# Four column groups in the mixed stage, four kinds of projections with the weights stationary, modulation chunks of 2048 rows, and the mixer's small steps at new tile numbers

## The chip, the cores and the metric

The kernel runs on one core of a Trainium2 chip. The metric is the device time of one execution in microseconds (us). TensorE (PE) multiplies, VectorE (DVE), ScalarE (ACT) and GpSimd (POOL) do the rest, and the queues of SyncE (SP) and POOL start the DMA transfers.

## What is computed

Two blocks over x (256 positions, 2048 channels), all in float32. Only the first one is touched by the change:

```python
mod = silu(c) @ w_ada + b_ada                 # w_ada is 2048 x 12288
sh1, sc1, gt1, sh2, sc2, gt2 = split(mod, 6)
h = rmsnorm(x, g_mix) * (1 + sc1) + sh1
z = h @ w_in                                  # pool, q, k, v, forget logits, lru x, lru y
y = concat(pool_mixer(zp), forgetting_attention(zq, zk, zv, zf), rg_lru_branch(zx, zy))
x = x + gt1 * (y @ w_out)
h = rmsnorm(x, g_ffn) * (1 + sc2) + sh2
x = x + gt2 * conv_glu_ffn(h)
```

The pool mixer is a banded product over positions and a map of each group; the attention has 8 heads of 128 (two halves of 4 heads) with a decay from a cumulative sum F of the forget logits; the lru branch is a causal convolution of width 4 over positions, two sigmoid gates from 128x128 blocks, a scan over positions, and a gelu of zy. Then comes a second block of two layers, whose first step, the projection of a memory (256 x 2048) to keys mk and values mv of each layer, is done at the front.

## The kernel before

All weights are streamed. A tile is 256 rows (two pieces of 128) by 512 columns, 512 KB. SP loads it into one of RING = 4 slots of `w_raw`; ACT rounds it to float32r (`w_hi`, L579 in the front), DVE subtracts for the rest (`w_lo`, L1679), and PE makes three products of each pair of pieces (L1039 to L1041): hi by hi, w_lo by hi, w_hi by lo. The activations are held transposed as `hT_hi` and `hT_lo` and are the stationary operand; a matmul has 512 moving columns of weights and gives rows of positions. So a tile costs 2 pieces x 2 blocks of positions x 3 = 12 matmuls. A slot is refilled when PE has used it: ACT splits tile g after PE is through tile g - 4.

The first 136 tiles are the front. They belong to 17 units of 8 tiles (`FRONT`): mk0, mv0, mk1 (tiles 0 to 23), then x, y and p interleaved (tiles 24 to 47, "the mixed stage"), q0, k0, v0, q1, k1, v1 (48 to 95), the four output groups o0 to o3 (96 to 127) and mv1 (128 to 135). A unit has 8 tiles because 2048 rows are 8 x 256. x and y are the two halves of the lru branch, p is the pool.

In the mixed stage, hT is rewritten for its next use piece by piece: piece s needs four numbers per channel block of the modulation. `w_ada` is read transposed in chunks of 128 outputs by 1024 rows, two per block of outputs: POOL starts each load (L475), DVE multiplies the chunk with silu(c) and sums it along the free dimension (`weigh`, L1606), the second half starting from the sum of the first. The first 64 halves (`EARLY`) are weighed from tile 2 to tile 39 and feed the eight pieces (`gain_stage`, `refill_mixed` on ACT, `mixed_low` on DVE); nine slots hold them. The other 96 that belong to the front are spread evenly from tile 44 to tile 130, with five slots. The last 32 are weighed in the feed-forward part.

Every engine runs one list of instructions written out by hand. `upto(t)` in an engine's list works through the tiles below t; the small steps stand between such calls. On PE: the transposes of each of x, y, q and k (8 of 128x128 each, L1074), the forget logits (L1191 to L1193), the pool products (L1207, L1226), the gates (L1217), the logits of the attention (L1152, L1153, first half after tile 68, second after 92), the transposes of the probabilities (L1161), the values (L1102), the broadcast of the output gate (L1116) and y_T (L1074). Where DVE has a step between tiles t and t+1, the `w_lo` of tile t+1 comes behind it.

After tile 112, SP also queues two loads for later stages (3.4 MB). DVE takes o0 (`residual`, L1669 and L1671) behind the `w_lo` of tile 113, and o3 behind that of tile 131; a row norm, PE transposes (L1092) and the feed-forward part hang on the latter.

Of the kernel before, what the change touches and what calls it, by code (L numbers as in the profile page):

```python
# [29 lines left out]
PARTS = 2  # L30
AH = D // PARTS
ADA_RING = 5
ADA_SLOTS = (14, 15, 16, 17, 18, 4, 5, 6, 7)
# [18 lines left out]
FRONT = ("mk0", "mv0", "mk1", "x", "y", "p", "q0", "k0", "v0", "q1", "k1", "v1", "o0", "o1", "o2", "o3", "mv1")  # L52
F_OUT = FRONT.index("o0")
F_X = FRONT.index("x")
BANK = {"mk0": 0, "mv0": 1, "mk1": 0, "x": 1, "y": 0, "p": 2, "q0": 1, "k0": 0, "v0": 1, "q1": 0, "k1": 1, "v1": 0,
        "o0": 1, "o1": 0, "o2": 1, "o3": 0, "mv1": 1}
BEFORE = [max((v for v in range(u) if BANK[FRONT[v]] == BANK[FRONT[u]]), default=None) for u in range(len(FRONT))]
F_TILES = [(u, j) for u in range(F_X) for j in range(GT)]
F_TILES += [(F_X + i, j) for j in range(GT) for i in range(3)]
F_TILES += [(u, j) for u in range(F_X + 3, F_OUT) for j in range(GT)]  # L60
# [16 lines left out]
CHUNKS = [(n, h) for n in range(len(BLOCKS)) for h in range(PARTS)]  # L77
EARLY = PARTS * M_GATE1
ADA_PLACE = [i % len(ADA_SLOTS) if i < EARLY else (i - EARLY) % ADA_RING for i in range(len(CHUNKS))]
ADA_TURN = [ADA_PLACE[:i + 1].count(p) for i, p in enumerate(ADA_PLACE)]  # L80
ADA_BEFORE = [max((v for v in range(i) if ADA_PLACE[v] == p), default=None) for i, p in enumerate(ADA_PLACE)]
# [100 lines left out]
def build(nc, t):  # L182
    with ExitStack() as ctx:
# [124 lines left out]
        zf, logf = view(16, S)[0:8, :], view(17, S)[0:8, :]  # L308
        wf_hi, wf_lo = view_r(5, KD, 8), view_r(5.5, KD, 8)
# [54 lines left out]
        ada_in = [sem(f"ada_in{i}") for i in range(len(ADA_SLOTS))]  # L364
# [59 lines left out]
        def _(sp):  # L424
# [3 lines left out]
            for g in range(FT):  # L428
# [41 lines left out]
        def _(pool):  # L470
            pool.wait_ge(mem_in[0], 16)
            for i in range(len(CHUNKS)):
                if ADA_BEFORE[i] is not None:
                    pool.wait_ge(ada_used, ADA_BEFORE[i] + 1)
                pool.dma_start(ada_at[ADA_PLACE[i]], t["w_ada"][i]).then_inc(ada_in[ADA_PLACE[i]], 16)  # L475
                if i == EARLY + 11:
                    pool.wait_ge(zf_ps, 1)
                    pool.dma_start(band, t["band"]).then_inc(band_in, 16)

            pool.wait_ge(lru_ps, 6)  # L480
# [12 lines left out]
        def _(act):  # L493
# [48 lines left out]
            front_dest = {"mk0": mk_tok[0], "mv0": mv[:, 0, :, :], "x": Zx, "y": Zy, "p": Zp, "q0": Zq[0], "k0": Zk[0],  # L542
                          "v0": Zv[0], "q1": Zq[1], "k1": Zk[1], "v1": Zv[1], "mk1": mk_tok[1], "mv1": mv[:, 1, :, :]}
# [1893 lines left out]
```

## Time and profile before

| | us |
|---|---|
| median of 3 runs (3099.75 to 3101.12) | 3100.82 |
| the profiled execution | 3100.88 |
| its span in the trace | 3099.1 |

PE is busy for 98% of the span, DVE for 65%, ACT for 48%. The span is the time from the first to the last instruction; 1.8 us lie around it. Times in the rows below are counted from its start. The duration of a matmul in the rows includes its way through the pipeline, so the price of one in a stream is the distance from its start to the next one's.

### The profile page before, as it was taken

How to read it: one execution, taken by the hardware profiler on the slowest of the kernel's cores; microseconds unless marked ns; L12 is line 12 of the kernel's file. 1: busy time of each engine (PE TensorE's matmuls, PEld its weight loads, DVE VectorE, ACT ScalarE, POOL GpSimd, SP SyncE). 2: the span in 40 equal slices, each digit the busy share in tenths (PEclk: the TensorE clock that was granted, in tenths of full speed). 3: DMA queues.
4: the chain of work that ended last, by engine and by line, in shares of the span. 5: the costliest groups of instructions: out<-in, count | busy, mean ns of one | idle time of the engine just before them, and what ended most of it. 6: DMA issues, size and time to landing. Idle time of an engine off the chain costs nothing.

```text
span 3099.1 us, 38332 instructions
## 1 busy us (share of the span) xinstructions
PE 3033.9 (98%) x14098; PEld 2523.6 (81%) x14098; DVE 1999.3 (65%) x2277; ACT 1496.7 (48%) x1769; POOL 104.8 (3%) x202
## 2 busy tenths in 40 slices
PE   6899998999999999999999999999999999999999
PEld 5677877888888888888888888888888888888887
DVE  7989888865665666775555565565475655565564
ACT  4555545444544444545444444544545444444543
POOL 2211111100000000000000000000000000000000
PEclk9999999999999999999999999999999999999999
DMA  9988896855556555554556545555455555555555
GB/s 396 387 321 301 315 376 248 341 189 189 184 183 195 187 189 186 166 182 164 193 173 191 177 162 191 169 191 186 167 183 170 192 175 193 171 165 191 170 183 190
DMA packets 179429, 657.11 MB, mean 212 GB/s; under 512 B 19904, under 2 KB 20192, under 8 KB 178528
## 3 DMA queue, kind: packets, MB, share of 16 engines
q1 hardware_dynamic: 151008, 551.28, 52.8%
q0 software_dynamic: 28288, 103.98, 8.9%
q8 instruction: 92, 1.51, 0.2%
q14 instruction: 41, 0.34, 0.0%
HBM read 653.09 MB, written 2.10 MB: 211 GB/s over the span
## 4 chain that ended last, share of the span: by engine, by line
PE 90%; DVE 5%; DMA 2%; issue 1%; ACT 1%; SPq 0%; DVEq 0%; ACTq 0%
PE pg L1039 28%; PE pg L1041 28%; PE pg L1040 28%; DVE R L1606 2%; DMA w_raw<-w 2%; PE pm L1074 1%; DVE w_lo L1679 1%; PE pm L1102 1%; PE pm L1492 1%; DMA R<-w_ada 1%; PE pm L1386 0%; ACT w_hi L579 0%; PE pm L1442 0%; PE pm L1083 0%; PE pm L1116 0%
## 5 line engine op out<-in xcount | busy, mean ns | idle before, releaser
L1541 DVE TENSOR_TENSOR w_lo<-w_raw,w_hi 128x1024 fp32r<-128x1024 f32 x888 | 1085.7, 1225 | 973.7 <-ACT w_hi L500 969.3
L500 ACT ACTIVATE w_hi<-w_raw 128x1024 fp32r<-128x1024 f32 x888 | 940.7, 1060 | 1329.9 <-PE pg L1041 1304.2
L1039 PE MATMUL pg<-w_hi,hT_hi 128*128 128x512 f32 x3200 | 1265.6, 396 | 52.5 <-DVE w_lo L1679 36.5
L1041 PE MATMUL pg<-w_hi,hT_lo 128*128 128x512 f32 x3200 | 1251.4, 391 | 0.0
L1040 PE MATMUL pg<-w_lo,hT_hi 128*128 128x512 f32 x3200 | 1251.0, 391 | 0.0
L1039 PEld LDWEIGHTS pg<-w_hi,hT_hi 128*128 128x128 f32 x3200 | 604.5, 189 | 183.5 <-issue 32.8
L1041 PEld LDWEIGHTS pg<-w_hi,hT_lo 128*128 128x128 f32 x3200 | 604.0, 189 | 127.3
L1040 PEld LDWEIGHTS pg<-w_lo,hT_hi 128*128 128x128 f32 x3200 | 604.8, 189 | 121.7
L1039 PE MATMUL pg<-w_hi,y_parts 128*128 128x512 f32 x864 | 337.6, 391 | 1.4 <-issue 1.4
L1041 PE MATMUL pg<-w_hi,y_parts 128*128 128x512 f32 x864 | 336.3, 389 | 0.0
L1040 PE MATMUL pg<-w_lo,y_parts 128*128 128x512 f32 x864 | 336.1, 389 | 0.0
L579 ACT ACTIVATE w_hi<-w_raw 128x1024 fp32r<-128x1024 f32 x140 | 147.5, 1059 | 174.8 <-PE pg L1041 85.4
L1679 DVE TENSOR_TENSOR w_lo<-w_raw,w_hi 128x1024 fp32r<-128x1024 f32 x140 | 170.4, 1220 | 53.4 <-ACT w_hi L579 52.9
L1039 PEld LDWEIGHTS pg<-w_hi,y_parts 128*128 128x128 f32 x864 | 162.2, 188 | 34.8 <-issue 1.8
L1041 PEld LDWEIGHTS pg<-w_hi,y_parts 128*128 128x128 f32 x864 | 162.2, 188 | 33.8
L1040 PEld LDWEIGHTS pg<-w_lo,y_parts 128*128 128x128 f32 x864 | 162.3, 188 | 33.2
L1606 DVE CUSTOM_DVE_ANT_0 R<-R,mod 128x1024 f32<-128x1024 f32 x96 | 122.8, 1280 | 4.5 <-DMA R<-w_ada 1.7
L1606 DVE CUSTOM_DVE_ANT_0 R<-R,vec_sb 128x1024 f32<-128x1024 f32 x96 | 122.7, 1279 | 0.9 <-DMA R<-w_ada 0.7
L475 POOL DMA_DIRECT2D R<-w_ada x192 | 101.5, 529 | 498.2 <-DVE mod L1606 490.7
L881 ACT ACTIVATE R<-pg,sc 128x512 f32<-128x512 f32 x124 | 77.7, 677 | 0.1
L1074 PEld LDWEIGHTS pm<-con_sb,R 128*128 128x128 f32 x448 | 51.2, 140 | 5.1
L1074 PE MATMUL pm<-con_sb,R 128*128 128x128 f32 x448 | 55.2, 272 | 0.0
(284 smaller groups left out, 1398.5 us busy)
## 6 DMA issues: line engine op xcount, KB each, us to landing
w_raw<-w SPq DMA_DIRECT2D x1028, 512.0 KB, 3.9
R<-w_ada POOLq DMA_DIRECT2D x192, 512.0 KB, 7.4
R<-mem_T SPq DMA_DIRECT2D x4, 512.0 KB, 10.2
x_rows<-x SPq DMA_DIRECT2D x1, 2048.0 KB, 16.2
R<-mem_T SPq DMA_DIRECT2D x1, 2048.0 KB, 12.0
out<-x_rows SPq DMA_DIRECT2D x4, 512.0 KB, 5.0
con_sb<-con SPq DMA_DIRECT2D x1, 1344.0 KB, 16.1
small_w_sb<-small_w POOLq DMA_DIRECT2D x2, 576.0 KB, 5.7
```

The costliest lines, as they stand in the source:

```text
L475: pool.dma_start(ada_at[ADA_PLACE[i]], t["w_ada"][i]).then_inc(ada_in[ADA_PLACE[i]], 16)
L500: act.activation(w_hi[:, g % RING, :, :].rearrange("p c n -> p (c n)"), raw[:, g % RING, :], ACT.Copy).then_inc(hi_done, 1)
L579: act.activation(w_hi[:, g % RING, :, :].rearrange("p c n -> p (c n)"), raw[:, g % RING, :], ACT.Copy).then_inc(hi_done, 1)
L881: i = act.activation(dest[:, tb, :], src[:, tb, :], func, scale=rs[:, tb:tb + 1])
L1039: pe.matmul(out, hi, w_hi[:, slot, c, :], start=start, stop=False)
L1040: pe.matmul(out, hi, w_lo[:, slot, c, :], start=False, stop=False)
L1041: return pe.matmul(out, lo, w_hi[:, slot, c, :], start=False, stop=stop)
L1074: i = pe.transpose(pm[b][:, c * S + tb * P:c * S + (tb + 1) * P], rows[:, tb, (2 * q + c) * P:(2 * q + c + 1) * P], ident)
L1102: i = pe.matmul(pm[tb][:, h * P:(h + 1) * P], PT[:, h, sb_, tb * P:(tb + 1) * P], v[:, sb_, h * P:(h + 1) * P], start=(sb_ == 0), stop=(sb ...
L1541: tt(flat(w_lo[:, g % RING, :, :]), raw[:, g % RING, :], flat(w_hi[:, g % RING, :, :]).bitcast(F32), ALU.subtract).then_inc(lo_done, 1)
L1606: dve.tensor_tensor_reduce(chunk, chunk, c_rows[:, h, :], 1.0, start, ALU.mult, ALU.add, mod[:, n:n + 1]).then_inc(ada_used, 1)
L1679: tt(flat(w_lo[:, g % RING, :, :]), raw[:, g % RING, :], flat(w_hi[:, g % RING, :, :]).bitcast(F32), ALU.subtract).then_inc(lo_done, 1)
```

## The change

- The order of the front is mk0, mk1, mv0, then y, p, q0, x interleaved in the mixed stage (tiles 24 to 55), k0, v0 and so on. q0 gets the PSUM banks of the small steps (`pm` 0 and 1).
- The units of `COLUMNS` (y, q0, x, k0, q1, k1) are made by `column_passes`: the weights (128x128) are the stationary operand and hT moves with 256 columns. So a tile is 2 pieces x 4 column blocks x 3 = 24 matmuls of 256 columns. The result is already transposed, and the 6 times 8 transposes, with their copies, go. ACT copies y, q0, k0, q1 and k1 from PSUM to where they are used, with the attention's scale for q; for x it applies the convolution's last tap and bias in the same copy.
- A block's modulation is one chunk of 2048 rows (1 MB): one `weigh` and one accumulated sum in place of two. A chunk takes two slots; where these are not neighbours it is loaded in two pieces. There are four places of 1 MB for the early ones, and five slots of 512 KB for the late ones.
- The 32 early chunks are weighed from tile 2 to 45. The 48 late ones of the front are spread unevenly (`LATE`): 9 over 13 tiles from 47, 9 over 25 from 60, 7 over 10 from 85, 10 over 18 from 95 and 13 over 18 from 113.
- DVE's first small steps, which wait for `vec`, stand behind the first tile. The keys of both memories are normed between tiles 14 and 23. The forget logits come after tile 55, the pool after 59, the gates after 61 and 65, the logits of the attention after 70 and 90; F is transposed after 67. Loads of `con1` and `pool_w` are started at tile 52 instead of 26, those of `b_f` and `front_w` at 44.

```diff
-PARTS = 2
-ADA_RING = 5
-ADA_SLOTS = (14, 15, 16, 17, 18, 4, 5, 6, 7)
+ADA_EARLY = (14, 16, 4, 6)
+ADA_LATE = (14, 15, 16, 17, 18)
-FRONT = ("mk0", "mv0", "mk1", "x", "y", "p", "q0", "k0", "v0", ...
+FRONT = ("mk0", "mk1", "mv0", "y", "p", "q0", "x", "k0", "v0", ...
+COLUMNS = ("y", "q0", "x", "k0", "q1", "k1")
+MIXED = 4
-        EARLY_FEEDS = [2 + 38 * i // EARLY for i in range(EARLY)]
+        LATE = ((47, 9, 13), (60, 9, 25), (85, 7, 10), (95, 10, 18), (113, 13, 18))
+        WEIGH_FEEDS = [2 + 45 * n // EARLY for n in range(EARLY)]
+        WEIGH_FEEDS += [at + span * i // count for at, count, span in LATE for i in range(count)]
...
+            def column_passes(out, k, slot, c, b):
+
+                hi, lo = (w[:, slot, c, b * P:(b + 1) * P] for w in (w_hi, w_lo))
+                pe.matmul(out, hi, hT_hi[:, k, :], start=k == 0 and b % 2 == 0, stop=False)
+                pe.matmul(out, hi, hT_lo[:, k, :], start=False, stop=False)
+                return pe.matmul(out, lo, hT_hi[:, k, :], start=False, stop=k == KD - 1 and b % 2 == 1)
...
-                        for tb in range(TB):
-                            i = passes(front_bank(u, tb), hT, k, tb, done % RING, c, k == 0, k == KD - 1)
+                        if FRONT[u] in COLUMNS:
+                            for b in range(4):
+                                i = column_passes(front_bank(u)[:, b // 2, b % 2 * S:(b % 2 + 1) * S], k, done % RING, c, b)
+                        else:
+                            for tb in range(TB):
+                                i = passes(front_bank(u, tb), hT, k, tb, done % RING, c, k == 0, k == KD - 1)
...
-            def weigh(i):
-                n, h = CHUNKS[i]
-                chunk = ada_at[ADA_PLACE[i]]
-                dve.wait_ge(ada_in[ADA_PLACE[i]], 16 * ADA_TURN[i])
-                start = V("b_ada")[:, n:n + 1]
-                if h:
-                    dve.wait_ge(ada_used, i)
-                    start = mod[:, n:n + 1]
-                dve.tensor_tensor_reduce(chunk, chunk, c_rows[:, h, :], 1.0, start, ALU.mult, ALU.add,
+            def weigh(n):
+                chunk = ada_at(n)
+                for at, _, _ in ada_loads(n):
+                    dve.wait_ge(ada_in[at], 16 * ada_turn(at, n))
+                dve.tensor_tensor_reduce(chunk, chunk, c_rows, 1.0, V("b_ada")[:, n:n + 1], ALU.mult, ALU.add,
                                          mod[:, n:n + 1]).then_inc(ada_used, 1)
...
-            transposes(Zx, (2, 3), lru_ps)
-            transposes(Zy, (0, 1), lru_ps)
-            transposes(Zq[0], (0, 1), T_ps)
-            transposes(Zk[0], (2, 3), T_ps)
-            attn_at(69, 0, Zv[0], 8, 0)
+            attn_at(71, 0, Zv[0], "k0", 0)
-            transposes(Zq[1], (0, 1), T_ps)
-            transposes(Zk[1], (2, 3), T_ps)
-            attn_at(93, 1, Zv[1], 12, 4)
+            attn_at(91, 1, Zv[1], "k1", 4)
```

## Rows read from the trace of the kernel before

**Rows 1.** The page: busy time of each engine.

```profile
PE 3033.9 (98%) x14098; PEld 2523.6 (81%) x14098; DVE 1999.3 (65%) x2277; ACT 1496.7 (48%) x1769; POOL 104.8 (3%) x202
```

**Rows 2.** Stretches: length, busy time of each engine, clock, DMA share, GB/s.

```profile
110.21:174.00 63.79, 52.23 (x218) 40.97 (x219) 62.09 (x88) 28.84 (x39) 11.59 (x22) 0.95 0.88 335
0.00:202.82 202.82, 164.27 (x728) 131.02 (x729) 171.54 (x253) 103.28 (x135) 41.93 (x83) 0.96 0.97 377
202.82:421.30 218.48, 214.63 (x1043) 179.52 (x1041) 192.91 (x266) 110.05 (x161) 35.98 (x68) 1.00 0.88 319
426.95:481.20 54.25, 54.25 (x228) 44.59 (x229) 54.08 (x70) 26.00 (x38) 10.02 (x19) 0.95 0.95 358
```

**Rows 3.** Waits of PE from 0 to 500 us: total, times, longest.

```profile
PE pg L1039 <- DVE w_lo L1679: 36.5, 13, 13.2
PE pg L1039 <- ACT R L584: 7.9, 1, 7.9
PE pg L1039 <- DVE R L1669: 5.5, 1, 5.5
PE pm L1161 <- ACT R L607: 3.5, 4, 1.9
```

**Rows 4.** Timeline of PE: first matmuls of tiles 24, 49 and 50.

```profile
110.21 0.47 PE L1039 MATMUL pg<-w_hi,hT_hi 128*128 128x512 f32 x1 [1.46 <-DVE w_lo L1679]
...
200.10 0.39 PE L1039 MATMUL pg<-w_hi,hT_hi 128*128 128x512 f32 x1
...
202.82 0.39 PE L1039 MATMUL pg<-w_hi,hT_hi 128*128 128x512 f32 x1
```

**Rows 5.** Timeline of PE: first and last of 48 matmuls with 8 stationary columns.

```profile
189.17 0.28 PE L1191 MATMUL pm<-hT_hi,y_parts 128*8 128x256 f32 x1
...
194.52 0.28 PE L1193 MATMUL pm<-hT_lo,y_parts 128*8 128x256 f32 x1
```

**Rows 6.** Timeline of PE: a run of transposes and one of plain float32 products, with what follows.

```profile
205.55 1.91 PE L1074 MATMUL pm<-con_sb,R 128*128 128x128 f32 x16
207.22 0.47 PE L1039 MATMUL pg<-w_hi,hT_hi 128*128 128x512 f32 x1
...
387.78 3.73 PE L1102 MATMUL pm<-R 128*128 128x128 f32 x32
391.26 0.48 PE L1039 MATMUL pg<-w_hi,hT_hi 128*128 128x512 f32 x1
```

**Rows 7.** Groups of DVE, 424.5 to 481.2 us: busy us, mean ns, idle.

```profile
L1679 DVE TENSOR_TENSOR w_lo<-w_raw,w_hi 128x1024 fp32r<-128x1024 f32 x19 | 23.2, 1220 | 5.8 <-ACT w_hi L579 5.8
L1606 DVE CUSTOM_DVE_ANT_0 R<-R,mod 128x1024 f32<-128x1024 f32 x10 | 12.8, 1280 | 0.1
L1606 DVE CUSTOM_DVE_ANT_0 R<-R,vec_sb 128x1024 f32<-128x1024 f32 x9 | 11.5, 1280 | 0.0
...
L1644 DVE TENSOR_TENSOR hT_lo<-R,hT_hi 128x512 fp32r<-128x512 f32 x7 | 4.8, 686 | 0.0
```

**Rows 8.** Timeline of DVE: two halves of a chunk, and the steps at tile 131.

```profile
412.89 1.28 DVE L1606 CUSTOM_DVE_ANT_0 R<-R,vec_sb 128x1024 f32<-128x1024 f32 x1
...
414.33 1.28 DVE L1606 CUSTOM_DVE_ANT_0 R<-R,mod 128x1024 f32<-128x1024 f32 x1
...
479.76 1.22 DVE L1679 TENSOR_TENSOR w_lo<-w_raw,w_hi 128x1024 fp32r<-128x1024 f32 x1
480.89 1.22 DVE L1669 TENSOR_TENSOR R<-pg,R 128x1024 f32<-128x1024 f32 x1
```

**Rows 9.** Timeline of ACT: it waits for the transfer of tile 113.

```profile
423.45 1.06 ACT L579 ACTIVATE w_hi<-w_raw 128x1024 fp32r<-128x1024 f32 x1 [9.01 <-DMA w_raw<-w]
```

**Rows 10.** DMA queues and issues, 20 to 100 us: q0 is POOL's, q1 SP's.

```profile
q0 software_dynamic: 5136, 18.72, 59.5%
q1 hardware_dynamic: 3259, 13.42, 41.8%
...
w_raw<-w SPq DMA_DIRECT2D x20, 512.0 KB, 7.3
```

More of the change, by code:

```diff
@@ L76, with ada_slots, ada_loads, ada_turn @@
 BLOCKS += [5 * KD + k for k in range(KD)]
[L77 to L81, printed above, removed]
+EARLY = M_GATE1
+def ada_slots(n):
+    if n < EARLY:
+        first = ADA_EARLY[n % len(ADA_EARLY)]
+        return (first, first + 1)
+    r = 2 * (n - EARLY)
+    return tuple(sorted(ADA_LATE[(r + h) % len(ADA_LATE)] for h in range(2)))
+def ada_loads(n):
+    a, b = ada_slots(n)
+    return [(a, 0, D)] if b == a + 1 else [(a, 0, AH), (b, AH, D)]
+def ada_turn(slot, n):
+    return sum(load[0] == slot for m in range(n + 1) for load in ada_loads(m))
+def ada_before(n):
+    return max((m for m in range(n) if set(ada_slots(m)) & set(ada_slots(n))), default=None)
 IN2 = 15
@@ L363, in build @@
         mem_in = [sem(f"mem_in{i}") for i in range(4)]
-        ada_in = [sem(f"ada_in{i}") for i in range(len(ADA_SLOTS))]
+        ada_in = {i: sem(f"ada_in{i}") for i in sorted(set(ADA_EARLY + ADA_LATE))}
         raw_in = [sem(f"raw_in{i}") for i in range(RING)]
@@ L471, in _ @@
             pool.wait_ge(mem_in[0], 16)
[L472 to L477, printed above, removed]
+            for n in range(len(BLOCKS)):
+                if ada_before(n) is not None:
+                    pool.wait_ge(ada_used, ada_before(n) + 1)
+                for at, first, last in ada_loads(n):
+                    pool.dma_start(slot(at, last - first), t["w_ada"][n][:, first:last]).then_inc(ada_in[at], 16)
+                if n == EARLY + 2:
+                    pool.wait_ge(hT_ready, P_MIX + GT)
                     pool.dma_start(band, t["band"]).then_inc(band_in, 16)
-            pool.wait_ge(lru_ps, 6)
+            pool.wait_ge(lru_ps, 2)
             for l in range(LAYERS):
@@ L1105, in outs, with heads_of @@
                     i.then_inc(o_ps, 1)
+            def heads_of(v):
+                return [v[:, h, :, :] for h in range(NH)]
             def y_T(occ, rows):
@@ L1151, in attn_at @@
                         out = pm[h][:, tb * S:(tb + 1) * S]
-                        pe.matmul(out, QK1[:, 0, h, tb * P:(tb + 1) * P], QK1[:, 1, h, :], start=True, stop=False)
+                        pe.matmul(out, Q1[occ][:, h, tb * P:(tb + 1) * P], K1[occ][:, h, :], start=True, stop=False)
                         i = pe.matmul(out, ident[:, forget + h:forget + h + 1].to_broadcast([P, P]), F_row,
@@ L1178, in _ @@
             pe.wait_ge(hn_ready, 1)
-            transposes(mk_tok[0], (1, 2), T_ps)
-            upto(34)
+            transposes(mk_tok[0], (0, 1), T_ps)
+            upto(23)
             pe.wait_ge(T_sb, 2)
@@ L1761, in _ @@
             mem_normed(0)
-            for s in range(4):
-                upto(20 + s)
-                gain_stage(s)
-            for s in range(3):
-                upto(24 + s)
-                mixed_low(s)
+            upto(20)
+            mem_squares(1)
+            gain_stage(0)
+            upto(21)
+            gain_stage(1)
+            upto(22)
+            gain_stage(2)
+            upto(23)
+            mem_normed(1)
+            upto(24)
+            mixed_low(0)
+            gain_stage(3)
```

415 lines of the change are left out of this document (209 added, 206 removed).

## Prediction, made before the changed kernel ran

> **What bounds the kernel now.** I read the page first: PE is busy for 98% of the span [rows 1], so outside of a few places only PE's own work counts. Then the stretches, the waits of PE, and its timeline tile by tile. In a stream, a 512-column matmul starts every 0.227 us; the tile that starts at 200.10 is followed by the next at 202.82 [rows 4], so a tile costs 2.72 us, 12 x 0.227. What PE does beyond 2.72 us per tile is small steps, waits and half clock. All that the change touches lies in the first 136 tiles, which end at about 510 us. I cut them into three stages.
>
> Stage A, 0 to 202.82 us, tiles 0 to 49. 50 tiles are 136 us. PE's first matmul waits until 13.2 us, and nearly all its other waits of the front are here: for `w_lo` (36.5 us with the first 13.2) and 7.9 us for a copy by ACT behind a late tile [rows 3]. What is behind them: DMA is busy for 97% of the stage at 377 GB/s, so it moved 76.5 MB; and DVE, busy for 62.09 of 63.79 us between 110 and 174 us, is the bound there [rows 2]. Tile 24 starts at 110.21, behind a `w_lo` [rows 4].
>
> Stage B, 202.82 to 421.30 us, tiles 50 to 111. PE is busy for 214.63 of 218.48 us at full clock; DMA 88%, DVE 192.91 us [rows 2]. The only waits are 3.5 us for the exponentials of the first attention half [rows 3] and 0.4 us.
>
> Stage C, from the end of tile 111. PE waits 5.5 us for o0's residual [rows 3], which stands behind the `w_lo` of tile 113, for whose transfer ACT waited 9.01 us [rows 9]: 3.4 MB were queued ahead of it. From then to tile 131 DVE is busy for 54.08 of 54.25 us [rows 2], its `w_lo` of tile 131 ends at 480.98, and PE starts that tile at 481.2. The residual of o3 follows at 480.89 [rows 8], and norm, transposes and the feed-forward part hang on it. So DVE is the bound of stage C.
>
> **The column products.** 48 tiles get 24 matmuls of 256 columns each instead of 12 of 512. No row has float32r with 128 stationary and 256 moving columns. With 8 stationary columns, 48 of them start between 189.17 and 194.52, 5.35/47 = 0.114 us apart [rows 5]: half of 0.227, so the price goes by moving columns, and 24 of them cost 2.73 us. What is open is the weight load of 128 columns for each, now 0.114 us apart. Two rows bound it: 16 transposes, each with its own load of 128 float32 columns, take 207.22 - 205.55 = 1.67 us, 0.104 each; 32 plain float32 products with 128 stationary columns take 391.26 - 387.78 = 3.48 us, 0.109 each [rows 6]. A load can thus follow a load within 0.104 us behind running matmuls, which is less than 0.114. I take 2.73 us per tile: nothing gained or lost. The ends: 0, or the load wholly in the open, 48 x 24 x 0.104 = +120 us.
>
> The Trainium skill (TensorE: Matmul & The Clock Gate, What overlaps and what doesn't) says that a weight load overlaps with running matmuls only when it goes to another row group. All loads here fill all rows. By that rule they would lie in the open and the change would cost the upper end just given. The trace disagrees for 512 columns: 0.227 us is twice the 0.114 us of matmuls whose load is nearly empty, so loads of 128 columns add nothing there [rows 4, 5].
>
> **What goes from PE in stage B.** 48 transposes x 0.104 = 5.0 us [rows 6], and four breaks of the stream, some 0.1 us each: -5.4. New places of the other steps add two or three breaks, +0.2. The 3.9 us of waits in the first attention half and before it: in the last nine tiles before, DVE had its convolution scan, gelu and 1.1 half chunks per tile at once. After, the logits come two tiles later, the scan stands behind them, and the chunks are 9 over 25 tiles: 0.36 x 2.36 = 0.85 us per tile instead of 1.1 x 1.29 = 1.42. Per tile DVE has 1.14 + 0.85 = 2.0 us of 2.72. I take all of these waits away, with 0.4 of breaks: -4.3. The forget logits and the rest only change place within or between the stages (I count them in both times). Sum B: -9.5, ends -5 (waits stay) and -12.
>
> **What a chunk costs DVE.** Half a chunk is 1.28 us for 1024 elements [rows 7], and with the sum's read 1.29 us of DVE in a row; the second half of a pair starts 414.33 - 412.89 = 1.44 us after the first [rows 8]. From 512 to 1024 elements a subtraction goes from 0.686 to 1.220 us [rows 7], so 1024 elements more cost 1.07 us and a full chunk 2.35, with the read 2.36, against 2.58 to 2.65 for the two halves.
>
> The Trainium skill (VectorE: DVE Perf Modes, The TRN2 errata) gives (N + 151)/0.96 ns for a float32 two-operand pass and says that the fixed part is paid per instruction. By that a chunk saves 0.16 us; our halves have a larger fixed part (1280 - 1070 = 210 ns), and the read goes too.
>
> **Stage A after.** In the time to tile 50, DVE was busy for 171.54 us, with 64 early and 11 late halves: 75 x 1.29 = 96.8. After, 32 + 5 chunks have to be weighed until there: 37 x 2.36 = 87.3. DVE's sum is 162.0. It was idle for 31.3 us before, 9.5 of it at first for `vec`; I keep two thirds, since the first wait is now for other transfers that come sooner and the early chunks are thinner (0.71 per tile against 0.84): 162 + 20 = 182. DMA: 54 tiles x 0.524 + 80 halves x 0.524 + 6.3 MB of others = 76.5 MB, which is just what the row gives. After: 54 tiles 28.3, 37 chunks 38.8, 2.5 chunks ahead 2.6, others 5.8: 75.5 MB, or 72.9 without those ahead. At the 409 GB/s of its full windows (I read 18.72 + 13.42 MB in 80 us as 402 [rows 10]) that is 178 to 187 us. PE alone: 13.2 + 136 + 7.4 + 1.7 for its small steps + some 10 at half clock = 168. So tile 50 starts at 182, DVE and DMA about level. Before it was 202.82, of which 48 x 0.114 = 5.45 were the forget logits that now come later: 197.4. Gain A: -15; ends -22 (half of DVE's rest goes) and -5 (DMA at its measured mean of 377 gives 193 without chunks ahead). The stall of 7.9 us is a part of this: mk1's bank is no longer the one that the mixed stage opens with.
>
> What is late next: nothing that PE sees until tile 113. 9 chunks over 13 tiles from 47 are 9 x 2.36 + 13 x 1.14 + 3 = 39 us of DVE against 13 x 2.72 + 5.45 = 40.8 of PE.
>
> **Stage C after.** Before, 19 halves stand from tile 113 on: 24.5 us. After 13 chunks: 30.7. Everything else of DVE stays, and it had no rest [rows 2, 7], so the residual of o3 and all behind it come 6.2 us later. The wait for tile 113 stays, its 3.4 MB are queued as before. DMA: 3 MB more in this stretch, 3.1/0.41 = 7.7 us, of which the idle 5% of 54 us hide 2.7. I take +6; ends 0 and +12. Chunks of the feed-forward part: DVE's saving there is hidden under PE.
>
> **Sum.** -15 - 9.5 + 6 = -18.5. Against the profiled execution's 3100.88 (span 3099.1 and 1.8 around it; the median is 3100.82) this gives 3082.4, so 3082.
>
> **Rivals.**
> - The tail isn't charged: DMA or PE leave DVE gaps that the trace does not show, or less stands in DVE's way after 113. Then 3100.9 - 24.5 = 3076. Against it: 0.17 us of idle in 54. Chance 0.15.
> - The first stage gives little: DMA stays its bound at its mean rate or the mixed pieces arrive late for four units. A = -2: -2 - 9.5 + 6 gives 3095. For it, the 97% of DMA. Chance 0.13.
> - The chunk transfers crowd out the tiles. In 20 to 100 us POOL's queue moved 18.72 MB and SP's 13.42, and a tile took 7.3 us to land [rows 10]; SP runs four tiles ahead, 10.9 us of PE. If rows twice as long give POOL's queue two shares, a tile takes about 7.3 x 3/2 = 11 us, and the three dense places (47, 85, 113) each lose some 3.7 us: 3093. The Trainium skill (DMA: Bandwidth & Descriptors, Arbitration) lets each engine take turns between queues by packets, which is this mechanism. Chance 0.08.
> - The other side: the loads are not hidden. The gains are 18.5 us; 18.5/1152 = 16 ns more per column matmul eat them, and wholly in the open they give 3202. Against it the two rows at 0.104 and 0.109; for it only that no row has this form. Chance 0.06.
>
> My forecast has 0.58. A measurement of this kernel tells 0.2%, 6.2 us. Faster by more: 0.58 x 0.97 + 0.15 + half of the third + 0.03 of the second = 0.78. Within: 0.13. Slower: 0.06 and 0.03 for a new wait, 0.09. The range goes from 3070 (A -22, B -10, C +1) to 3097 (A -2, B -8, C +6), which leaves out the column loads and little more.
>
> **What would show it.** Column matmuls 0.114 us apart; tile 50 at 180 to 186 us; no transposes between tiles 50 and 91 but those of probabilities and y; a full chunk of 2.35 us; `w_lo` of tile 131 with PE waiting for it, and the way from tile 113 to 131 some 6 us longer. Spacing of 0.13 or more, or PE waits for `w_lo` between tiles 50 and 111, would make it wrong.

## The result, and the profile after

The changed kernel takes 3131.35 us (median of 4 runs, 3129.29 to 3133.32); the kernel before took 3100.86 in the runs beside it. The ratio is 1.010, 95% interval 1.0084 to 1.0116: slower, where I had forecast 3082 and faster. The profiled execution took 3129.29 us with a span of 3127.5, 28.4 more than before.

The page of the changed kernel, which answers to [rows 1], with the two groups and the issue that changed most:

```profile
PE 3045.6 (97%) x14626; PEld 2554.1 (82%) x14626; DVE 1984.8 (63%) x2085; ACT 1491.5 (48%) x1758; POOL 60.9 (2%) x119
...
L1639 DVE CUSTOM_DVE_ANT_0 R<-R,vec_sb 128x2048 f32<-128x2048 f32 x96 | 225.4, 2348 | 40.7 <-DMA R<-w_ada 40.4
...
L614 ACT ACTIVATE w_hi<-w_raw 128x1024 fp32r<-128x1024 f32 x140 | 147.5, 1059 | 228.3 <-DMA w_raw<-w 136.9
...
R<-w_ada POOLq DMA_DIRECT2D x83, 1024.0 KB, 8.0
```

DVE has 192 instructions fewer [rows 1], and a full chunk costs 2348 ns, the 2.35 us of my estimate. The new thing stands at the end of the second row: DVE waits 40.4 us for chunks.

The same stages as in the prediction, from the starts of tiles 24, 50, 112, 131 and 140 (us). "Before" for tile 50 is without the 5.45 us of forget logits, "after" for stage B as well:

| stretch | before | after | moved by | forecast |
|---|---|---|---|---|
| A: to tile 50 | 197.4 | 201.5 | +4.1 | -15 |
| B: tile 50 to the end of tile 111 | 218.5 | 222.2 | +3.7 | -9.5 |
| C: end of tile 111 to tile 131 | 59.9 | 78.6 | +18.7 | +6 |
| tile 131 to tile 140 | 38.9 | 38.8 | 0 | 0 |
| tile 140 to the end | 2579.0 | 2581.0 | +2.0 | 0 |

Waits between 0 and 560 us, of the changed kernel (total, times, longest); the rows with `w_lo`, with L1683 (the residual) and with L1207 (the exponentials) answer to [rows 3], where these cost 36.5, 5.5 and 3.5:

```profile
PE pg L1069 <- DVE w_lo L1693: 33.3, 16, 5.4
PE pg L1069 <- DMA con_sb<-con: 9.6, 1, 9.6
PE pg L1069 <- DVE R L1683: 8.4, 1, 8.4
PE pg L1158 <- DVE w_lo L1693: 5.6, 6, 3.0
PE pm L1158 <- DVE w_lo L1693: 4.8, 3, 3.4
PE pm L1069 <- DVE w_lo L1693: 4.1, 3, 3.1
PE pm L1207 <- ACT R L650: 1.6, 1, 1.6
...
DVE w_lo L1693 <- ACT w_hi L614: 62.7, 31, 11.0
DVE R L1639 <- DMA R<-w_ada: 30.0, 11, 6.5
...
ACT w_hi L614 <- DMA w_raw<-w: 136.9, 51, 11.9
...
POOL R L512 <- DVE hT_lo L1658: 10.2, 1, 10.2
```

The same three waits in the kernel before, over the same stretch:

```profile
DVE w_lo L1679 <- ACT w_hi L579: 52.9, 36, 5.8
DVE R L1606 <- DMA R<-w_ada: 2.4, 3, 1.3
...
ACT w_hi L579 <- DMA w_raw<-w: 84.0, 42, 9.0
```

DVE's wait for chunks went from 2.4 to 30.0 us, ACT's for tiles from 84.0 to 136.9. Both are transfers, although the kernel moves the same bytes. Stretches of the changed kernel (columns as in [rows 2]): stages A, B and tiles 112 to 131, then two short ones inside A:

```profile
0.00:201.47 201.47, 163.62 (x909) 139.28 (x909) 160.34 (x174) 99.33 (x130) 20.20 (x42) 0.95 0.92 357
201.47:429.07 227.60, 222.70 (x1390) 201.34 (x1390) 185.13 (x198) 108.59 (x154) 20.68 (x40) 0.98 0.84 310
437.63:507.71 70.08, 58.60 (x229) 45.72 (x229) 61.97 (x58) 24.91 (x37) 8.42 (x16) 0.92 0.85 321
...
80.00:90.00 10.00, 10.00 (x55) 8.53 (x54) 7.26 (x7) 6.91 (x10) 0.59 (x2) 1.00 0.64 230
...
111.68:178.00 66.32, 61.29 (x438) 56.83 (x439) 61.20 (x59) 31.63 (x42) 7.38 (x14) 1.00 0.99 389
```

In A, DVE's work is 160.34 us, as forecast (162), but its idle time is 201.47 - 160.34 = 41.1 us, where I had put 20 beside it. DMA is at 0.64 from 80 to 90 us and at 0.99 from 111.68 on: in the thin part there was bandwidth to spare, and no free place to load into (whether this cost anything, the runs below tell). In C, DVE's work grew by 61.97 - 54.08 = 7.9 us, close to the forecast; the other 8 us are idle time that stage C did not have before, 7.7 of it waits for chunks, while DMA's share fell from 0.95 to 0.85. So there DVE waits for transfers and DMA is not full: the transfers start too late.

Where the waits fall, in the timelines of PE, DVE, POOL and ACT:

```profile
182.06 0.50 PE L1069 MATMUL pm<-w_hi,hT_hi 128*128 128x512 f32 x1 [3.10 <-DVE w_lo L1693]
201.47 0.58 PE L1158 MATMUL pm<-hT_hi,w_hi 128*128 128x256 f32 x1 [3.44 <-DVE w_lo L1693]
437.63 0.79 PE L1069 MATMUL pg<-w_hi,hT_hi 128*128 128x512 f32 x1 [8.40 <-DVE R L1683]
638.81 0.49 PE L1069 MATMUL pg<-w_hi,y_parts 128*128 128x512 f32 x1 [2.92 <-DVE R L1948]
...
197.31 2.35 DVE L1639 CUSTOM_DVE_ANT_0 R<-R,vec_sb 128x2048 f32<-128x2048 f32 x1 [3.75 <-DMA R<-w_ada]
209.30 2.35 DVE L1639 CUSTOM_DVE_ANT_0 R<-R,vec_sb 128x2048 f32<-128x2048 f32 x1 [6.55 <-DMA R<-w_ada]
464.68 2.35 DVE L1639 CUSTOM_DVE_ANT_0 R<-R,vec_sb 128x2048 f32<-128x2048 f32 x1 [4.72 <-DMA R<-w_ada]
...
189.31 1.05 POOL L509 DMA_DIRECT2D R<-w_ada  x2 [17.34 <-DVE mod L1639]
200.57 0.53 POOL L512 DMA_DIRECT2D R<-band  x1 [10.22 <-DVE hT_lo L1658]
201.09 1.04 POOL L509 DMA_DIRECT2D R<-w_ada  x2
...
434.12 1.06 ACT L614 ACTIVATE w_hi<-w_raw 128x1024 fp32r<-128x1024 f32 x1 [11.89 <-DMA w_raw<-w]
```

Chunk 34 is the first with only five slots: POOL can load it when chunk 32 is weighed, and starts nothing for 17.34 us. DVE then waits 3.75 us for it, just ahead of tile 50. POOL next stands for 10.22 us ahead of the load of `band`; the loads of chunk 35 and later are behind it in its queue. Chunk 35 then keeps DVE waiting for 6.55 us, and `w_lo` of the following tiles is behind that. In B, tiles 50 to 52 take 5.28, 6.19 and 4.44 us in place of 2.88 each, +7.3 with the half clock that the rests bring (0.50 granted between 201.47 and 206.76).

The column products, PE's timeline in the changed kernel, the first piece of a tile:

```profile
323.55 0.28 PE L1158 MATMUL pg<-hT_hi,w_hi 128*128 128x256 f32 x1
323.67 0.28 PE L1159 MATMUL pg<-hT_lo,w_hi 128*128 128x256 f32 x1
323.79 0.28 PE L1160 MATMUL pg<-hT_hi,w_lo 128*128 128x256 f32 x1
```

They start 0.120 us apart, not 0.114, so such a tile takes 24 x 0.120 = 2.88 us and 48 of them 7.7 us more than the row form. The stretch from 320 to 330 us, in the columns of [rows 2]:

```profile
320.00:330.00 10.00, 10.00 (x86) 10.00 (x86) 6.56 (x8) 2.19 (x3) 0.53 (x1) 1.00 0.83 304
```

The weight loads (PEld) are busy for all of it; before they were for 179.52 of stage B's 218.48 us [rows 2]. By itself this does not show that they set the pace.

### The profile page after: what moved, and what is told of

The parts are those of the page before. It is cut to its first block, busy times and chain, and to the rows that moved or that the text cites. A ratio compares the mean times of both kernels' runs of the same rounds, so it can differ in the third digit from the quotient of the medians.

```text
span 3127.5 us, 39020 instructions
## 1 busy us (share of the span) xinstructions
PE 3045.6 (97%) x14626; PEld 2554.1 (82%) x14626; DVE 1984.8 (63%) x2085; ACT 1491.5 (48%) x1758; POOL 60.9 (2%) x119
## 4 chain that ended last, share of the span: by engine, by line
PE 85%; DVE 7%; DMA 6%; ACT 1%; issue 1%; SPq 0%; POOL 0%; DVEq 0%; ACTq 0%
PE pg L1069 25%; PE pg L1071 25%; PE pg L1070 25%; DMA w_raw<-w 3%; DVE R L1639 3%; DMA R<-w_ada 3%; DVE w_lo L1693 2%; PE pm L1104 1%; PE pm L1132 1%; PE pm L1529 1%; PE pg L1159 1%; PE pg L1160 1%; PE pg L1158 1%; DVE w_lo L1578 1%; PE pm L1423 0%
## 5 line engine op out<-in xcount | busy, mean ns | idle before, releaser
L1069 PE MATMUL pg<-w_hi,hT_hi 128*128 128x512 f32 x3008 | 1190.6, 396 | 54.0 <-DVE w_lo L1693 33.3
L1070 PE MATMUL pg<-w_lo,hT_hi 128*128 128x512 f32 x3008 | 1176.8, 391 | 0.0
L1071 PE MATMUL pg<-w_hi,hT_lo 128*128 128x512 f32 x3008 | 1176.6, 391 | 0.0
L1069 PEld LDWEIGHTS pg<-w_hi,hT_hi 128*128 128x128 f32 x3008 | 568.6, 189 | 179.5 <-DVE w_lo L1693 24.0
L1071 PEld LDWEIGHTS pg<-w_hi,hT_lo 128*128 128x128 f32 x3008 | 568.1, 189 | 119.8
L614 ACT ACTIVATE w_hi<-w_raw 128x1024 fp32r<-128x1024 f32 x140 | 147.5, 1059 | 228.3 <-DMA w_raw<-w 136.9
L1639 DVE CUSTOM_DVE_ANT_0 R<-R,vec_sb 128x2048 f32<-128x2048 f32 x96 | 225.4, 2348 | 40.7 <-DMA R<-w_ada 40.4
L1158 PE MATMUL pg<-hT_hi,w_hi 128*128 128x256 f32 x320 | 92.8, 290 | 5.6 <-DVE w_lo L1693 5.6
L1159 PE MATMUL pg<-hT_lo,w_hi 128*128 128x256 f32 x320 | 91.3, 285 | 0.0
L1160 PE MATMUL pg<-hT_hi,w_lo 128*128 128x256 f32 x320 | 91.2, 285 | 0.0
L509 POOL DMA_DIRECT2D R<-w_ada x109 | 57.5, 529 | 562.3 <-DVE mod L1639 557.3
```

The lines of the kernel that those rows point to most:

```text
L614: act.activation(w_hi[:, g % RING, :, :].rearrange("p c n -> p (c n)"), raw[:, g % RING, :], ACT.Copy).then_inc(hi_done, 1)
L1069: pe.matmul(out, hi, w_hi[:, slot, c, :], start=start, stop=False)
L1070: pe.matmul(out, hi, w_lo[:, slot, c, :], start=False, stop=False)
L1071: return pe.matmul(out, lo, w_hi[:, slot, c, :], start=False, stop=stop)
L1158: pe.matmul(out, hi, hT_hi[:, k, :], start=k == 0 and b % 2 == 0, stop=False)
L1159: pe.matmul(out, hi, hT_lo[:, k, :], start=False, stop=False)
```

## The experiments

My theory after this reading: (1) the modulation's chunks arrive late, because a place of 1 MB is refilled only when both of its 512 KB slots are free, and because the dense places (47, 85, 113) ask for more bytes and DVE time than their tiles last; (2) the column products cost 7.7 us for their weight loads. The rival was the prediction's third: rows of 8 KB give POOL's queue more of the engines than the tiles get. Times are medians; the kernel before ran beside each group at 3099.7 to 3100.9.

**e1_half_chunks.** The changed kernel with halves of 1024 rows again, nine places and later five, both halves weighed where the whole was:

```diff
-            for n in range(len(BLOCKS)):
-                if ada_before(n) is not None:
-                    pool.wait_ge(ada_used, ada_before(n) + 1)
...
+            for i in range(len(CHUNKS)):
+                if ADA_BEFORE[i] is not None:
+                    pool.wait_ge(ada_used, ADA_BEFORE[i] + 1)
```

> The changed kernel, with its modulation chunks halved again (1024 rows, two sums per block, nine places early and five late, as before), each pair weighed where the whole chunk was. Theory G (the ring is too coarse: in five half slots only two whole chunks fit, a slot is refilled only after its weigh, so DMA idles and then DVE waits in order for a chunk): faster than the changed kernel, DVE's 30.0 us of waits for w_ada fall below 12, time 3110 to 3120 against 3131. Theory D (what costs is the dense feeding places, 13 chunks in 18 tiles, whatever their size): DVE has 0.25 us more per chunk, time 3131 to 3145. Theory C (column matmuls): no change, 3128 to 3136.

3121.84 us (3120.11 to 3122.98), ratio 1.0067 (1.005 to 1.0084): 9.5 less than the change, a third of the loss, although DVE's work is larger again. That is 2 us short of the range given for theory G; DVE's wait for chunks falls from 30.0 to 12.1 us.

**e2_two_loads.** Every chunk as two transfers with rows of 4 KB, all else as in the change:

```diff
-    return [(a, 0, D)] if b == a + 1 else [(a, 0, AH), (b, AH, D)]
+    return [(a, 0, AH), (b, AH, D)]
```

> The changed kernel, whole chunks of 2048 rows weighed at once, but each loaded by two transfers with rows of 4 KB in place of one with rows of 8 KB. Theory P (long rows give POOL's queue more than its share, so weight tiles land late): as fast as with half chunks or near it, 3112 to 3122, ACT's 136.9 us of waits for w_raw fall under 110. Theory G and theory D: the space and the order stay as they are, so 3129 to 3135.

3139.46 us (3134.98 to 3144.86), ratio 1.0122 (1.0105 to 1.0139): 8 us slower, not faster, and ACT's waits for tiles rise to 163.2 us where theory P wanted them under 110. So the length of the rows does not explain the loss. But its trace shows that the rival is not empty. From 7 to 19 us both queues are at work all the time; packets, MB and share of each, first in the changed kernel, then in this one:

```profile
q0 software_dynamic: 367, 2.74, 54.3%
q1 hardware_dynamic: 772, 2.23, 46.9%
...
q1 hardware_dynamic: 951, 2.88, 60.8%
q0 software_dynamic: 516, 1.92, 40.0%
```

With rows of 8 KB POOL's queue (q0) moves 2.74 MB in these 12 us, with 4 KB 1.92 MB, and tile 2 lands at 24.2 us instead of 19.6. All six kernels of this study with rows of 8 KB (five with the change, and e8) have 2.68 to 2.75 MB there and tile 2 at 23.5 to 24.3 us; the eleven with rows of 4 KB have 1.92 to 2.03 MB and 19.2 to 19.9 us. From 100 to 180 us the issues of tiles in the kernel before, in the changed kernel and in this one are:

```profile
w_raw<-w SPq DMA_DIRECT2D x23, 512.0 KB, 7.0
...
w_raw<-w SPq DMA_DIRECT2D x24, 512.0 KB, 8.7
...
w_raw<-w SPq DMA_DIRECT2D x26, 512.0 KB, 7.8
```

So stage A is faster here: tile 49 starts at 186.31 us, against 195.12 in the changed kernel (191.93 and 193.43 in e3 and e4, which differ from it only later). From tile 50 on it is slower. There a chunk's landing time counts, because only two chunks are under way: from its first issue to its last landing chunks 34 to 43 take 8.9 us on average instead of 7.6, DVE's wait for chunks goes from 30.0 to 53.8 us in the front, and tile 140 to the end takes 2589.9 us instead of 2581.0. The 8 us are the difference of two effects.

**e3_even_feed.** The 48 late chunks spread evenly:

```diff
-        LATE = ((47, 9, 13), (60, 9, 25), (85, 7, 10), (95, 10, 18), (113, 13, 18))
+        LATE = ((47, 48, 84),)
```

> The changed kernel with its 48 late chunks spread evenly, one every 1.75 tiles from tile 47 on, in place of the five densities. Theory D: from tile 112 to 131 it takes 62 to 66 us in place of 81, the stalls at tiles 50 and 52 shrink, and the time is 3112 to 3120. Theory G: the lookahead of two chunks is short only where chunks come faster than one per 8 us, so most of the last stretch is won back too, but some stalls of single chunks stay: 3116 to 3124. Theory C: 3131.

3113.02 us (3108.24 to 3114.08), ratio 1.0037 (1.0024 to 1.0049): -18.3. Tile 50 starts at 194.68 and tile 131 at 489.24. Tiles 112 to 131 of this kernel:

```profile
430.29:489.24 58.95, 56.08 (x228) 44.49 (x229) 54.99 (x52) 24.98 (x37) 6.31 (x12) 0.95 0.88 334
```

And DVE's wait for chunks, 0 to 560 us:

```profile
DVE R L1639 <- DMA R<-w_ada: 32.3, 15, 7.0
```

The stretch is 58.95 us instead of 70.08, 54.25 before. DVE's wait for chunks stays at 32.3 us: the even feed removes the crowd, not the late start of each load.

**e4_band_later.** POOL takes the load of `band`, with its wait, two chunks later:

```diff
-                if n == EARLY + 2:
+                if n == EARLY + 4:
```

> The changed kernel; POOL's wait for the last mixed piece, ahead of the load of the band matrix, stands two chunks later in its queue, so that it no longer holds back the chunks weighed at tiles 51 and 52. If the wait is what makes the stalls before tiles 50 and 52 (3.4 and 3.0 us, with half clock after each): 3124 to 3128 and tile 56 some 5 us earlier. If the DMA bandwidth there is the bound anyway: 3130 to 3133.

3127.62 us (3124.0 to 3128.48), ratio 1.0083 (1.0066 to 1.01): -3.7, and POOL no longer waits for `hT_lo`. A real cost, and a small one.

**e5_early_dense.** e3 and e4, and the early chunks packed as the halves were before:

```diff
-        WEIGH_FEEDS = [2 + 45 * n // EARLY for n in range(EARLY)]
+        WEIGH_FEEDS = [2 + 38 * n // EARLY for n in range(EARLY)]
```

> The changed kernel with the even late feeding, POOL's wait two chunks later, and the 32 early chunks weighed from tile 2 to 38 in place of 2 to 45. The even feeding and the later wait alone: some 3109 to 3111. If the first stage was slow because thin early chunks left DMA idle between 55 and 90 us (73% and 64% busy) and the mixed stage had to catch up at 3.2 us per tile: tile 50 comes 4 to 9 us earlier than with the even feeding (194.9) and the time is 3101 to 3107. If DMA's idle time there has another cause: 3109 to 3112.

3107.89 us (3102.88 to 3110.8), ratio 1.0023 (1.0012 to 1.0034). e3 and e4 alone would add up to 3109.3; what the denser early feed gives is 1.4 us, inside the spread of the runs. Tile 50 starts at 194.76, where e3 had 194.68, and not 4 to 9 us earlier, although DMA is at 0.74 from 80 to 90 us instead of 0.60: the thin early feed is not what makes stage A slow.

**e6_old_modulation.** The changed kernel with all of the old modulation: halves, its places, its even feeding, its place of the wait for `band`. The columns and the four groups stay.

```diff
-        LATE = ((47, 9, 13), (60, 9, 25), (85, 7, 10), (95, 10, 18), (113, 13, 18))
-        WEIGH_FEEDS = [2 + 45 * n // EARLY for n in range(EARLY)]
+        EARLY_FEEDS = [2 + 38 * i // EARLY for i in range(EARLY)]
+                weighs.setdefault(EARLY_FEEDS[i] if late < 0 else 44 + 87 * late // 96, []).append(i)
...
-                if n == EARLY + 2:
+                if i == EARLY + 11:
```

> The changed kernel with the modulation wholly as before: half chunks, nine and five places, weighed at the tiles of the kernel before; the columns, the four groups and the new places of the small steps stay. If the loss is all in how the chunks are cut and placed, what is left is 48 tiles at 2.88 us in place of 2.72 (+7.7), the transposes gone (-5.4), a fuller mixed stage and fewer waits: 3093 to 3100, faster than 3100.9. If columns and four groups cost by themselves: 3103 to 3110.

3098.69 us (3096.61 to 3099.13), ratio 0.9994 (0.9984 to 1.0003). All of the loss is gone, so it lies in the modulation; columns and regrouping together are worth nothing that can be told from zero.

**e7_cols64.** 64 stationary columns in place of 128 in the column products, so half of the rows of those six groups is left out:

```diff
-                hi, lo = (w[:, slot, c, b * P:(b + 1) * P] for w in (w_hi, w_lo))
+                hi, lo = (w[:, slot, c, b * P:b * P + WIDE] for w in (w_hi, w_lo))
+                out = out[0:WIDE]
```

> The changed kernel with half of the stationary columns left out in every column matmul (64 in place of 128, so half of the rows of those six groups is not computed); 256 moving columns as before. If the distance of 0.120 us is the weight load's: it falls to 0.114, and a column tile to 2.73 us. If it is a price of the form (256 moving columns, reads of hT): it stays at 0.120.

One execution: 3123.98 us, span 3122.2, 5.3 below that of the change; 1152 x 0.0065 = 7.5 were due if nothing else took it up. The starts in its PE timeline:

```profile
320.88 0.28 PE L1160 MATMUL pg<-hT_hi,w_hi 128*64 128x256 f32 x1
320.99 0.28 PE L1161 MATMUL pg<-hT_lo,w_hi 128*64 128x256 f32 x1
321.11 0.28 PE L1162 MATMUL pg<-hT_hi,w_lo 128*64 128x256 f32 x1
```

They are 0.1135 us apart on average, and a tile takes 2.72. So 256 moving columns cost what I took, and the 0.0065 above it go with the 128 stationary columns. Halving them also halves the rows that are written. But the 512-column matmuls of the row form write all 128 rows at the same rate per column (0.227 is twice 0.1135, [rows 4]), which leaves the load. PEld is busy for 10.00 of 10 us in this kernel too, so that figure tells nothing; a load takes 134 ns in its rows, and 192 ns with 128 columns.

**e8_before_whole.** The kernel before with nothing of the change but whole chunks, in the change's places and by its rule, fed evenly as the halves were (against the kernel before):

```diff
-ADA_RING = 5
-ADA_SLOTS = (14, 15, 16, 17, 18, 4, 5, 6, 7)
+ADA_EARLY = (14, 16, 4, 6)
+ADA_LATE = (14, 15, 16, 17, 18)
...
-    ada = [w_ada[h * AH:(h + 1) * AH, BLOCKS[n] * P:(BLOCKS[n] + 1) * P].T for n, h in CHUNKS]
+    ada = [w_ada[:, n * P:(n + 1) * P].T for n in BLOCKS]
```

> The kernel before with one thing of the change: whole chunks of 2048 rows, four early places and two and a half late ones, each weighed where its second half was; its order, rows and transposes stay. Theory G (coarse ring): slower than before by 3 to 12 us, with waits of DVE for w_ada in the dense places and 3 to 5 us in the feed-forward part, 3104 to 3113. If whole chunks are what they were priced at (0.25 us of DVE less for each): 3088 to 3100.

3115.25 us (3112.56 to 3116.4), ratio 1.0047 (1.003 to 1.0064): +15 with an even feed and no columns, 2 us above the range of theory G. Tile 50 starts at 203.57 (before 202.82), tile 131 at 488.04 (481.20); from tile 140 to the end it takes 2585.7 us against 2579.0. DVE's wait for chunks in the front:

```profile
DVE R L1631 <- DMA R<-w_ada: 24.7, 10, 8.3
```

**e9_halves_even, e10_halves_early_end, e11_con_later.** Half chunks in the changed kernel, early ones thin (to tile 45) and late ones even, POOL's wait for `band` three chunks later; then the late ones done by tile 122; or a load of 1.3 MB that SP queued at tile 112 put off to 128:

```diff
+        HALF_FEEDS = [2 + 44 * i // EARLY for i in range(EARLY)]
+        HALF_FEEDS += [47 + 84 * i // 96 for i in range(96)]      # e9, e11
+        HALF_FEEDS += [47 + 76 * i // 96 for i in range(96)]      # e10
...
-                    sp.dma_start(con[:, 2 * P:], t["con"][:, 2 * P:]).then_inc(late_in, 16)
+                if g == 128:                                      # e11
+                    sp.dma_start(con[:, 2 * P:], t["con"][:, 2 * P:]).then_inc(late_in, 16)
```

> The changed kernel with half chunks in nine and five places, the early halves weighed from tile 2 to 45 as the whole chunks of the change were, the late 96 spread evenly from tile 47 to 130, and POOL's wait for the band three chunks later. If cutting and placing are independent parts of the loss (halves -9.5, even feeding -18.3, later wait -3.7 against 3131.4) and add up: 3100. If the late places and the wait overlap, and the old modulation (3098.7) is about the floor that the other parts allow: 3096 to 3102. If early thin feeding costs with half chunks too: later than the old modulation by 3 or more.

> The last one with the late halves at tiles 47 to 122 in place of 47 to 130, so that DVE has none in the last eight tiles before the residual of o3. If DVE is the bound from tile 113 to 131 (54.1 of 54.3 us busy before): tile 131 comes 5 to 9 us sooner after tile 113 only if DMA and DVE have room between tiles 50 and 112 (1.26 halves per tile): 3090 to 3096. If that stretch becomes the bound in its place: 3098 to 3106.

> The first kernel of this call; the 1.3 MB load of the constants for the second block stands at tile 128 of SP's queue in place of 112. If the wait for o0's residual at tile 112 is the queue of 3.4 MB ahead of tile 113: the wait shrinks by 1.3 MB/0.41 = 3.3 us and, with less time at half clock, the time falls by 3 to 5 us. If it is the chunks of POOL's queue: no change within 1 us.

e9: 3095.57 us (3092.94 to 3097.26), ratio 0.9985 (0.9976 to 0.9995). e10: 3090.17 (3089.18 to 3092.32), 0.9971 (0.996 to 0.9982). e11: 3091.14 (3089.64 to 3094.36), 0.9974 (0.9963 to 0.9984). In e10 tiles 131 to 140 take 32.05 us instead of e9's 39.37: DVE has no chunks left when the residual of o3 comes. In e11 the transfer that ACT waited 9.01 us for [rows 9] is hardly late, and PE's wait for the residual at tile 112 is gone. Its ACT at tile 113:

```profile
416.30 1.06 ACT L585 ACTIVATE w_hi<-w_raw 128x1024 fp32r<-128x1024 f32 x1 [1.50 <-DMA w_raw<-w]
```

**e12_fine_ring.** Whole chunks, weighed as in the change and fed as in the change. But each is loaded in two halves of 512 KB, and POOL waits for each half's own slot:

```diff
-                if ada_before(n) is not None:
-                    pool.wait_ge(ada_used, ada_before(n) + 1)
-                for at, first, last in ada_loads(n):
+                for at, first, last in sorted(ada_loads(n), key=lambda load: freed(load[0])):
+                    if freed(at):
+                        pool.wait_ge(ada_used, freed(at))
```

> The kernel with two loads per whole chunk (3139.5), where POOL's queue now starts each half load as soon as its own 512 KB place is free, not when both are: 2.5 chunks ahead in place of 2, one weigh of 2048 rows as before. Theory G (the ring is too coarse): a third or more of what half chunks give comes back, 3126 to 3134. If it is the single weigh of 2.35 us that blocks DVE's queue and waits for the later of two halves: 3136 to 3142.

3112.7 us (3110.07 to 3115.1), ratio 1.0041 (1.0027 to 1.0056): 26.8 below e2, which has the same transfers and only the coarse wait. This is the coarse refill by itself, and twice the most that I expected of it. The 18.7 below the change hold two edits, this one and the two loads of e2. Up to chunk 33 both slots of a place come free together, so the fine wait changes nothing there, and tile 49 starts at 186.57 as in e2 (186.31). It acts from chunk 34 on, whose first half POOL starts at 166.2 us: tile 49 takes 4.51 us, where e2 has 8.59 and the change 6.35. Of the 14.2 us by which the span is shorter than the changed kernel's, 8.6 lie ahead of tile 49 and are those of the two loads.

**e13_fine_even.** e12, e3 and e4 together: whole chunks, all columns, fine refill, even feed. Its edits are those shown for the three.

> The changed kernel with whole chunks in two loads, each 512 KB place refilled as soon as it is free (3112.7 by itself), and the late chunks spread evenly with POOL's wait two chunks later (even feeding alone: 3113.0). If the coarse ring and the dense places are two names for one loss (with 2.5 chunks ahead density does not matter, with even density 2 chunks are enough): 3108 to 3113. If they add: 3098 to 3104.

3093.58 us (3091.94 to 3096.26), ratio 0.998 (0.997 to 0.999): 37.8 below the change, where the three alone add up to 18.7 + 18.3 + 3.7 = 40.7. So they nearly add, and it is 4 us below the range I had given for that. DVE's wait for chunks in the front:

```profile
DVE R L1642 <- DMA R<-w_ada: 9.7, 7, 3.7
```

And its first 190 us, in the columns of [rows 2]:

```profile
0.00:190.00 190.00, 162.54 (x928) 140.04 (x929) 161.60 (x176) 98.58 (x129) 39.79 (x80) 0.97 0.99 382
```

With DVE's work the same, DMA is at 0.99 instead of 0.92, and tile 50 starts at 187.66 instead of 201.47; 6.6 of these 13.8 us e2 has as well.

**e14_all_three.** The two edits of e10 and e11 on e9.

> Half chunks fed early from 2 to 45, late from 47 to 122, and the 1.3 MB of constants at tile 128 of SP's queue: the two best changes together (3090.2 and 3091.1, from 3095.6). The wait at tile 112 and the backlog at 131 are at different places; if they add: 3084 to 3087. If DMA after 112 is the common bound: 3088 to 3091.

3087.97 us (3086.68 to 3091.15), ratio 0.9964 (0.995 to 0.9978). It has the lowest median of the study, though its interval overlaps those of e10 and e11. The two steps give 7.6 us where alone they gave 5.4 and 4.4, which falls between the two ranges I gave; whether they share a wait stays open.

**e15_before_fine.** e8 with the edit of e12, the fine refill.

> The kernel before with whole chunks (3115.3), loaded in two and each 512 KB place refilled as soon as it is free. If the ring is the cause there too: half or more of its loss of 15 us comes back, 3100 to 3108. If a chunk of 2048 rows costs by its size (one weigh of 2.35 us, later of two loads): 3111 to 3118.

3104.26 us (3102.58 to 3106.52), ratio 1.0014 (1.0005 to 1.0024): 11 of the 15 us that whole chunks cost the kernel before come back with the two edits together. By the traces only 1.2 us of this lie ahead of tile 50 and 5.8 behind tile 140, so here it is mostly the refill. Of the other 4 the trace shows a PE wait of 2.0 us in the feed-forward part that the kernel before does not have; that the rest is the weigh of 2.35 us in front of whatever DVE does next is not shown.

## Why the prediction was wrong, point by point

**What a chunk costs DVE: right.** 2.348 us measured, 2.35 forecast, and DVE's sum of stage A too (160.34, forecast 162).

**Stage A, -15 forecast, +4.1 measured: the step that failed.** DVE's work was right, and what I put beside it was wrong: of its 31.3 us of idle time I kept 20 ("two thirds"), and after the change it had 41.1. DMA moved 357 GB/s on average where I had divided by 409. A gain of 15 us had to come out of PE's waits ahead of tile 50 for the most part, and these only went from 38.4 to 37.7. The runs show three reasons; the places are read from one profiled execution each, and kernels that are the same up to tile 47 differ by 3 us there.

- Rows of 8 KB. With 4 KB (e2, e12, e13) tile 49 starts at 186.31, 186.57 and 184.91, with 8 KB (the change, e3, e4) at 195.12, 191.93 and 193.43. I had this as my third rival, and had priced it at other places.
- "2.5 chunks ahead" is two: with five slots and two per chunk, waited for together, chunk 34 waits for the weigh of chunk 32, 17.34 us. The fine wait takes tile 50 from 194.90 (e2) to 191.08 (e12).
- The dense feed right behind it. With the even feed tile 49 takes 2.75 us (e3, e13) instead of 6.35.

The thin early chunks, with DMA at 0.64 from 80 to 90 us, are not among them: e12 has 0.62 there and is early at tile 49, and e5 with a denser feed gains nothing. Even e13, with tile 50 at 187.66, did not reach 182, the rest of DVE being larger than the 20 us I took (190 - 161.60 = 28.4 in its row).

**"Nothing that PE sees until tile 113": wrong.** I compared DVE's and PE's sums for tiles 47 to 59 and not when the transfers could start: 9 chunks and 13 tiles in 13 x 2.72 + 5.45 = 40.8 us are 9.4 + 6.8 MB, 398 GB/s, so DMA must not stand still, and it was at 0.66 from 180 to 190 us and at 0.81 from 200 to 210. And I had not listed what is queued behind POOL's wait for `hT_lo`, which is 10.22 us long; e4 prices it at 3.7, and takes tiles 50 to 52 from 15.9 to 10.2 us, most of their +7.3. These, together with the column products (+4.6 on this stage's 29 tiles), made +3.7 of stage B's -9.5. The transposes did go (-5.4 by the rows), and the waits for the exponentials fell from 3.5 to 1.6, half of what I took. PE waits for `w_lo` between tiles 50 and 111 were one of my signs of being wrong.

**The column products, 0 forecast, +7.7 measured: a term mis-sized.** The spacing is 0.120, between my 0.114 and the 0.13 at which I said I would be wrong. I had a load following a load in 0.104 and 0.109 [rows 6] and concluded that it hides. It does mostly. But those rows were other forms (128 moving columns, plain float32), and they did not bound this one: here a load for every 256 columns costs 0.0065 us, and e7, with half the columns to load, returns to 0.1135. The Trainium skill (TensorE: Matmul & The Clock Gate, What overlaps and what doesn't) would have put the load wholly in the open; 0.120 instead of 0.114 + 0.104 says that here it overlaps, and is not free.

**Stage C, +6 forecast, +18.7 measured: the direction right, the size not.** DVE's added work was right (7.9 against 6.2). I had priced the 3 MB more as hidden but for the queue's own length; in fact the chunks come late, DVE waits 7.7 us for them, and the 3.4 MB ahead of tile 113 cost 2.9 more than before. e3 takes 11.1 of the 15.8 us of tiles 112 to 131 back, e13 13.6.

**The feed-forward part, 0 forecast, +2.0.** "Hidden under PE" holds but for one place, where `down_out` stands behind a whole weigh, which itself had waited 2.4 us for its chunk: PE waits 2.9 us at 638.81. e8 has the same 2.9 on the kernel before, e12 with the fine wait 1.0.

**The rivals.** None came as stated. The nearest was that the first stage gives little (3095); but its reason, DMA at its mean rate, leaves out that DMA stood idle for want of a free place. The crowding by 8 KB rows is real, with tile 2 at 24.2 us instead of 19.6 and some 7 us at tile 49, but not where I had put it: the dense places stalled by the number of places, and shorter rows made them worse (e2). The clearly open loads (3202) did not occur. What decided it, that fewer and larger places leave a shorter lookahead, was not on my list.

What stays open: how the 4.7 us of tile 2 and the 7 us of tile 49 hang together (e8, with rows of 8 KB, has lost 4 us at tile 3 and none at tile 12), what of stage A's gain in e2 is the length of the rows and what the number of loads (the two always change together here), and what of the last 4 us of e15 is the length of a weigh and what the extra transfers.

## What to carry to other kernels

Transfers of twice the size use a ring of the same bytes worse: five places held 2.5 chunks as halves and two as wholes. Work out for each load the moment at which its place comes free, not only bytes over bandwidth, and wait for each piece of a place by itself: with the same loads that alone was worth 26.8 us here (e2 to e12), and with the two loads 18.7 against the change. An experiment that changes the shape of the transfers can gain in one stage and lose in another (e2), so read it stage by stage and not by its time alone. Before steps are bunched, add up the bytes as well as the engine time that fall into each bunch, and list what stands behind every wait in the queue that issues the loads.

## What the runs showed of the hardware

- A stream of float32r matmuls of 128 stationary and 256 moving columns runs at 0.120 us each, at 0.1135 with 64 stationary columns, while 512 moving columns take 0.227 [rows 4]. So a load of 128 columns is no longer hidden in full at 256 moving columns, and a tile takes 6% longer.
- Two queues with work all the time (7 to 19 us): with rows of 8 KB POOL's moved 2.74 MB and SP's 2.23, with two loads of 4 KB rows in place of one it moved 1.92 and SP's 2.88, and tile 2 landed 4.7 us earlier. So the queue with rows twice as long (and half as many loads) moved more, at the cost of the other one.
- From 100 to 180 us, with DMA nearly full, a tile landed 8.7 us after its issue beside 8 KB rows and 7.8 beside 4 KB rows (e2). A chunk in two loads took 8.9 us from its first issue to its last landing instead of 7.6 (chunks 34 to 43).
